# Hybrid encoder layer on one core: the down-projection of the 1024-token sequence as seven block products

## The chip, the cores and the metric

The program runs on one core of a Trainium2 chip. The metric is the device time of one execution in microseconds, lower is better. The engines of the core are TensorE (PE; its weight loads are listed as PEld), VectorE (DVE), ScalarE (ACT), GpSimd (POOL) and SyncE (SP), which here issues nearly all DMAs.

## The reference, cut to what matters

One encoder layer is applied, with the same parameters, to a prompt of 256 tokens and a sample of 1024 tokens. The change concerns its last part, the gated feed-forward network:

```
h2 = rmsnorm(x, pre_ffn_norm)
a, gate = split(h2 @ w_ffn_up, 2)          # 1024 -> 2 x 2816 features
a = centred_depthwise_conv(a, w, b)        # three taps along the tokens
f = gelu(a) * gate                         # 2816 features
x = x + rmsnorm(f @ w_ffn_down, post_ffn_norm)   # 2816 -> 1024
```

All of it is float32. Before it come the norm, the input projections, windowed attention, a bidirectional mLSTM, their gated merge and an output projection, which are as they were.

## The kernel before

Activations are kept transposed, features on partitions, tokens in columns; both sequences stand side by side as 1280 columns. A matrix product in float32 is made of three float32r matmuls: an operand is split into a high part (a rounded copy) and a low part (operand minus high), and high x high, high x low and low x high are added in PSUM. The helper `dense` (L2808) issues these three for every tile of 128 features: L2816, L2817 and L2818. So a weight that is loaded needs its high part (ScalarE, `unit_hi_ffn`, L1319) and its low part (GpSimd, `unit_lo`, L1232, which overwrites the raw weight in place), and an activation from DRAM likewise its high part (ScalarE, `pair_hi`, L1518) and its low part (DVE, `pair_lo`, L2649).

**Up stage.** 22 items, one for each tile of 128 of the 2816 features, each with the a and the gate columns of that tile. Six tiles of the first token half are done ahead, in the front; the 16 items that follow cover both halves of the tokens (c = 0 and 1), the last six, called lone items here, only the second. An item already uses the seven-product scheme with a 2 x 2 division: sums of weights are made by DVE (`block_sums`, L2548 to L2551, `last_block_sum`, L2558), the sums of operands exist. Each item is seven products of 12 matmuls per half (320 or 322 columns). DVE and ScalarE evacuate and add products (L2664, L2682, L2692, L2701), and do the convolution (L2514, L2517), gelu (L1403) and gating (L2710, L2711). SP then stores f to DRAM (`store_f`).

**Down stage.** f comes back from DRAM in three groups of tokens, `GROUPS_DOWN`: columns 0 to 400, 400 to 840 and 840 to 1280. For each group and each of eight output tiles k, `down_part` (in three parts of 8, 8 and 6 feature tiles) adds up 22 x 3 matmuls of 400 or 440 columns. In the last group the third parts stand behind all others, and those of output tiles 4 to 7 are made in two pieces of 224 and 216 columns. A weight unit of 8 tiles (512 KB) is loaded for every part and group again, through a ring of four slots (`ffn_slot`, `load_ffn`, L964): SP issues the load when the unit four before has been used. The chain behind a load is ScalarE's high part, GpSimd's low part, TensorE.

The outputs are evacuated and squared by ScalarE, the squares added by DVE (L2715), summed over features by a matmul against ones (L3347, L3375), and ScalarE makes the norm's factor of the sum (Ln and Exp, L1583 and L1585). DVE scales and adds the residual (`final`, `final_last`, L2726 to L2769), for the last group with GpSimd's help (L1309), and SP stores.

**What sets the order.** Every engine's program is written out by hand, in sequence. Engines wait for one another by semaphores; SP issues its DMAs in the order of its program, and a wait in it holds back all later ones. SP's DMAs are one queue (q1).

## Time and profile before

| | |
|---|---|
| three runs | 2429.69, 2430.98, 2431.22 us |
| median | 2430.98 us |
| profiled execution, span from first to last instruction | 2428.8 us |
| its own device time | not listed apart; the three runs lie 0.9 to 2.4 us above the span |
| TensorE busy, of the span | 98% |
| GpSimd, DVE, ScalarE busy | 51%, 55%, 38% |
| DMA moved | 245.23 MB, 101 GB/s on average |

In the profile the engines' busy times come first, then 40 slices of the span, DMA queues, the chain of work that ended last, and groups of instructions by line with what ended the idle time before them. Timelines list instructions by start; a matmul's record reaches over the start of the next one, so its length is not its cost, and the distance of starts is. In tables by stretch each engine's busy time is followed by the number of its instructions in brackets.

### The profile page before, as it was taken

How to read it: one execution, taken by the hardware profiler on the slowest of the kernel's cores; microseconds unless marked ns; L12 is line 12 of the kernel's file. 1: busy time of each engine (PE TensorE's matmuls, PEld its weight loads, DVE VectorE, ACT ScalarE, POOL GpSimd, SP SyncE). 2: the span in 40 equal slices, each digit the busy share in tenths (PEclk: the TensorE clock that was granted, in tenths of full speed). 3: DMA queues.
4: the chain of work that ended last, by engine and by line, in shares of the span. 5: the costliest groups of instructions: out<-in, count | busy, mean ns of one | idle time of the engine just before them, and what ended most of it. 6: DMA issues, size and time to landing. Idle time of an engine off the chain costs nothing.

```text
span 2428.8 us, 36204 instructions
## 1 busy us (share of the span) xinstructions
PE 2390.4 (98%) x13658; PEld 2179.4 (90%) x13658; DVE 1333.2 (55%) x2368; ACT 912.9 (38%) x1865; POOL 1238.1 (51%) x1548
## 2 busy tenths in 40 slices
PE   7999999999999999999999999999999999999998
PEld 6888888888888888888888899999999999999997
DVE  6623467334662356544776634997656568723323
ACT  5212444224432244324543112554333434543432
POOL 3145530445205641165544368795545456977664
PEclk9999999999999999999999999999999999999999
DMA  3133211321113211223355444332222224465552
GB/s 136 51 102 92 68 38 27 107 94 48 41 37 104 89 51 31 78 77 122 122 165 165 139 148 146 104 109 72 71 71 66 72 68 136 140 212 179 193 179 91
DMA packets 139190, 245.23 MB, mean 101 GB/s; under 512 B 11768, under 2 KB 85848, under 8 KB 139016
## 3 DMA queue, kind: packets, MB, share of 16 engines
q1 hardware_dynamic: 99368, 215.76, 26.8%
q10 hardware_dynamic: 39648, 27.15, 4.2%
q8 instruction: 109, 1.79, 0.3%
q14 instruction: 65, 0.53, 0.1%
HBM read 186.18 MB, written 56.61 MB: 100 GB/s over the span
## 4 chain that ended last, share of the span: by engine, by line
PE 87%; DVE 6%; DVEq 2%; POOL 2%; issue 1%; ACT 1%; DMA 1%; POOLq 0%; ACTq 0%
PE ps L2816 22%; PE ps L2818 22%; PE ps L2817 21%; PE ps L2862 3%; PE ps L2864 3%; PE ps L2863 3%; PE ps L3042 2%; PE ps L2952 2%; PE ps L2967 2%; PE ps L3062 2%; PE ps L2944 1%; PE ps L3075 1%; PE ps L3076 1%; PE ps L2934 1%; POOL unit_l L1232 1%
## 5 line engine op out<-in xcount | busy, mean ns | idle before, releaser
L2816 PE MATMUL ps<-ht_h,unit_h 128*128 128x512 f32 (+1 forms) x1408 | 508.9, 361 | 0.3 <-issue 0.3
L2818 PE MATMUL ps<-ht_h,unit_l 128*128 128x512 f32 (+1 forms) x1408 | 499.0, 354 | 0.0
L2817 PE MATMUL ps<-ht_l,unit_h 128*128 128x512 f32 (+1 forms) x1408 | 498.8, 354 | 0.0
L1102 POOL TENSOR_TENSOR unit_h<-unit_raw,colt 128x256 fp32r<-128x256 f32 x320 | 203.6, 666 | 353.1 <-DMA unit_raw<-w 352.8
L1232 POOL TENSOR_TENSOR unit_l<-unit_raw,unit_h 128x256 fp32r<-128x256 f32 x312 | 275.6, 916 | 97.0 <-ACT unit_h L1319 96.5
L2818 PEld LDWEIGHTS ps<-ht_h,unit_l 128*128 128x128 f32 x1408 | 266.2, 189 | 37.1
L2816 PEld LDWEIGHTS ps<-ht_h,unit_h 128*128 128x128 f32 x1408 | 266.6, 189 | 36.2 <-issue 0.7
L2817 PEld LDWEIGHTS ps<-ht_l,unit_h 128*128 128x128 f32 x1408 | 266.6, 189 | 35.8 <-issue 0.5
L1106 POOL TENSOR_TENSOR unit_l<-unit_raw,unit_h 128x256 fp32r<-128x256 f32 x320 | 245.6, 798 | 11.7 <-issue 0.4
L2816 PE MATMUL ps<-operands,unit_h 128*128 128x320 f32 (+1 forms) x740 | 230.9, 312 | 1.5 <-POOL sum_l L1272 1.0
L2818 PE MATMUL ps<-operands,unit_l 128*128 128x320 f32 (+1 forms) x740 | 229.7, 310 | 0.0
L2817 PE MATMUL ps<-operands,unit_h 128*128 128x320 f32 (+1 forms) x740 | 229.6, 310 | 0.0
L1272 POOL TENSOR_TENSOR unit_l<-unit_raw,unit_h 128x256 fp32r<-128x256 f32 x164 | 151.4, 949 | 94.9 <-DVE unit_raw L2551 94.9
L2816 PE MATMUL ps<-f,unit_h 128*128 128x440 f32 (+3 forms) x552 | 193.1, 350 | 0.9 <-POOL unit_l L1232 0.9
L2817 PE MATMUL ps<-f,unit_h 128*128 128x440 f32 (+3 forms) x552 | 192.4, 349 | 0.0
L2818 PE MATMUL ps<-f,unit_l 128*128 128x440 f32 (+3 forms) x552 | 192.3, 348 | 0.0
L1272 POOL TENSOR_TENSOR sum_l<-sum_raw,sum_h 128x256 fp32r<-128x256 f32 x132 | 133.1, 1028 | 101.4 <-DVE sum_raw L2558 87.0
L1148 POOL TENSOR_TENSOR bw<-bw,mask 128x256 f32<-128x256 f32 x40 | 29.3, 735 | 288.9 <-DMA bw<-exponent_rows_scratch 288.8
L1319 ACT ACTIVATE unit_h<-unit_raw 128x1024 fp32r<-128x1024 f32 (+1 forms) x84 | 83.4, 997 | 174.6 <-DMA unit_raw<-w 174.6
L2816 PE MATMUL ps<-operands,sum_h 128*128 128x320 f32 (+1 forms) x456 | 142.1, 312 | 1.4 <-POOL sum_l L1272 1.4
L2816 PEld LDWEIGHTS ps<-operands,unit_h 128*128 128x128 f32 x740 | 139.5, 188 | 3.7 <-POOL unit_l L1272 2.3
L2818 PE MATMUL ps<-operands,sum_l 128*128 128x320 f32 (+1 forms) x456 | 141.5, 310 | 0.0
(341 smaller groups left out, 5434.5 us busy)
## 6 DMA issues: line engine op xcount, KB each, us to landing
unit_raw<-w SPq DMA_DIRECT2D x197, 512.0 KB, 3.6
bw<-exponent_rows_scratch ACTq DMA_DIRECT2D x40, 256.0 KB, 3.8
unit_raw<-w SPq DMA_DIRECT2D x24, 384.0 KB, 3.0
f_raw<-f_scratch SPq DMA_DIRECT2D x10, 880.0 KB, 5.3
gate_scratch<-g_st SPq DMA_DIRECT2D x28, 256.0 KB, 3.6
f_scratch<-cv SPq DMA_DIRECT2D x22, 320.5 KB, 2.2
ym_scratch<-y_st ACTq DMA_DIRECT2D x40, 128.0 KB, 1.9
ya_scratch<-ya_st ACTq DMA_DIRECT2D x40, 128.0 KB, 2.5
```

Source lines behind the costliest of these rows:

```text
L1102: nc.gpsimd.tensor_tensor(unit_h[:, slot, k:k + 2], unit_raw[:, slot, k:k + 2], one_col.unsqueeze(2).to_broadcast([P, 2, P]), ALU.mult)
L1106: last = nc.gpsimd.tensor_tensor(unit_l[:, slot, k:k + 2], unit_raw[:, slot, k:k + 2], unit_h[:, slot, k:k + 2].bitcast(F32), ALU.subtract)
L1232: last = nc.gpsimd.tensor_tensor(unit_l[:, slot, k:k + 2], unit_raw[:, slot, k:k + 2], unit_h[:, slot, k:k + 2].bitcast(F32), ALU.subtract)
L1272: last = nc.gpsimd.tensor_tensor(lo[:, k:k + 2], raw[:, k:k + 2], hi[:, k:k + 2].bitcast(F32), ALU.subtract)
L1319: nc.scalar.activation(unit_h[:, slot, 0:k], unit_raw[:, slot, 0:k], ACT.Identity).then_inc(s_wh, 1)
L2816: mm(out_ap, wh, hi(k + k_first), start=first and k == 0, stop=False, skip_group_check=skip)
L2817: mm(out_ap, wh, lo(k + k_first), start=False, stop=False, skip_group_check=skip)
L2818: ins = mm(out_ap, wl, hi(k + k_first), start=False, stop=last and k == kts - 1, skip_group_check=skip)
L2862: mm(ps[:, bank, :], ht_h[:, k, t], unit_h[:, 0:4, k], start=k == 0, stop=False)
L2863: mm(ps[:, bank, :], ht_h[:, k, t], unit_l[:, 0:4, k], start=False, stop=False)
L2864: ins = mm(ps[:, bank, :], ht_l[:, k, t], unit_h[:, 0:4, k], start=False, stop=k == KT - 1)
L2952: ins = mm(ps[:, 3 + d, 0:DH + 1], qw[:, d, dt], c_st[:, d, dt], start=False, stop=dt == 1)
```

## The change

Only the down stage is new, and what prepares it. The prompt's 256 columns stay a direct product. The sample's 1024 tokens are halved (512 columns, `BT`), features are taken in pairs of tiles (even and odd, `HT` = 11 pairs) and output tiles in pairs p and p + 4 (`PAIRS` = 4). That is a 2 x 2 by 2 x 2 product: A11, A12, A21, A22 are blocks of the weight (even and odd feature tiles against output tile p, then against p + 4), B11, B12, B21, B22 of f (even and odd tiles, first and second token half). Seven products replace eight: A11 B11, A12 B21, S1 T1, S2 T2, S4 B22, S3 T3, A22 T4, where S1 = A21 + A22, S2 = S1 - A11, S3 = A11 - A21, S4 = A12 - S2 and T1 = B12 - B11, T3 = B22 - B12, T2 = B22 - T1, and T4 from B21 and T2.

1. **Token sums (T).** The sums are made by DVE from f as it lies in DRAM and go back to DRAM (`side_sum_scratch`). A round takes one feature pair and half of its columns: two loads into `stage`, four additions of 256 columns, one store of 512 KB. Six pairs and the weight sums of p = 0, 16 rounds, are made in the up stage, one round per item from item 1 to 16 (`ROUNDS`); the other five pairs, ten rounds, in the down stage, two per step (`ROUNDS_LATE`).
2. **First part of the down stage, by feature pairs.** Twelve steps: for each p, slices of 3, 4 and 4 feature pairs (`SLICES`). A step loads two units, the A21 and A22 tiles of the slice and the A11 and A12 tiles. TensorE makes the prompt's product with both (12 matmuls of 256 columns for a feature pair) and A11 B11 and A12 B21 with the second (6 of 512). While the raw weights are there, DVE makes S1 to S4 of the slice (`weight_sums`, eight additions, from step 2 on) and SP stores them (`weight_sum_scratch`); GpSimd may write a unit's low part over it only after the sums that read it.
3. **Second part, product by product.** Twenty blocks (`BLOCKS_DOWN`): for each of S1 T1, S2 T2, S4 B22, S3 T3, A22 T4, the four p, one block of 11 tiles from DRAM in three places of their own, 33 matmuls of 512 columns; ScalarE makes its high part, GpSimd its low part (six subtractions). The last two blocks are made in two halves of 256 columns. Token operands come in pieces (`SIDE_PIECES`, `piece_hi`, `piece_lo`) into two areas in turn.
4. DVE adds products from PSUM to what is kept in SBUF; squares, sums and norms are made as before by groups (prompt, second token half, first half in two quarters).
5. In lone items 1 to 3, and at the end of the last item, pieces of 1536, 2048 or 512 columns are split in place of pairs of 800. Four pieces more (4096 columns) follow the last item on ScalarE and DVE.

The diff, cut to its core:

```diff
-GROUPS_DOWN = [(0, 400), (400, 840), (840, T)]
...
+HT = FT // 2
+PAIRS = KT // 2
+BT = (T - SEQ_A) // 2
+HALF = BT // 2
+SUBS = [*range(FRONT // 2, HT), *range(FRONT // 2)]
+SLICES = [(0, 3), (3, 7), (7, HT)]
+STEPS = PAIRS * len(SLICES)
+U_END = U_DOWN + 2 * STEPS
+BLOCK_AT = {"A11": 0, "A12": 1, "A21": 2, "A22": 3}
+S_POS = {"S2": 0, "S4": 1, "S3": 2, "S1": 3}
+T_POS = {"T1": 0, "T3": 1, "T4": 2, "T2": 3}
+DOWN = [("S1", "T1"), ("S2", "T2"), ("S4", "B22"), ("S3", "T3"), ("A22", "T4")]
+BLOCKS_DOWN = PAIRS * len(DOWN)
...
+ROUNDS = [("S", 0, 2), ("S", 2, 4)] + [("T", m, r) for m in range(6) for r in range(2)] + [("S", 4, 6), ("S", 6, 7)]
+ROUNDS_LATE = [("T", m, r) for m in range(6, HT) for r in range(2)]
+LATE_FIRST = 2
+FIRST_SUMS = 2
+
...
+            def load_round(rounds, r, n):
+
+                kind, a, b = rounds[r]
+                if kind == "S":
+                    sp.dma_start(stage[n][:, :, 0:(b - a) * P], wdn[0, :, :, a * P:b * P].rearrange("b p c -> p b c")
+                                 ).then_inc(s_tl, 16)
+                    return
+                for k in range(2):
+                    src = f_d[2 * SUBS[a] + k, :, SEQ_A:T].rearrange("p (h r t) -> p h r t", h=2, r=2)
+                    sp.dma_start(stage[n][:, 2 * k:2 * k + 2], src[:, :, b]).then_inc(s_tl, 16)
...
+            def store_sums(n):
+
+                p, (a, b) = n // len(SLICES), slice_of(n)
+                for h, (c, d) in enumerate(((a, a + 2), (a + 2, b))):
+                    sp.wait_ge(w_sum, sums_done(n, 2 + h))
+                    sp.dma_start(s_d[p, :, :, c * P:d * P].rearrange("b p c -> p b c"), s_stage[h][:, :, 0:(d - c) * P]
+                                 ).then_inc(s_sst, 16)
...
+            for n in range(3, STEPS):
+                load_ffn(U_DOWN + 2 * n)
+                store_sums(n - 1)
+                load_ffn(U_DOWN + 2 * n + 1)
+                m = n - 2 - LATE_FIRST
+                if 0 <= m < late:
+                    for h in range(2):
+                        store_round(ROUNDS_LATE, 2 * m + h, h)
+                if 0 <= m + 1 < late:
+                    sp.wait_ge(s_tst, stored_rounds(len(ROUNDS), m + 1))
+                    for h in range(2):
+                        load_round(ROUNDS_LATE, 2 * (m + 1) + h, h)
...
+                if j >= U_DOWN + 2 * FIRST_SUMS:
+                    pool.wait_ge(w_sum, sums_done((j - U_DOWN) // 2, (1, 3)[j % 2]))
...
+            for n in range(5, 9):
+                piece_lo(n)
+            late = {0: (9,), 1: (10, 11, 12, 13, 14), 10: range(N_FIRST, N_FIRST + 3)}
+            for n in range(STEPS):
...
+                    V.tensor_tensor(x11, x12, x11, ALU.subtract)
+                    V.tensor_tensor(x12, x22, x12, ALU.subtract)
+                    dve.drain()
+                    V.tensor_tensor(x22, x22, x11, ALU.subtract)
+                    dve.drain()
+                    V.tensor_tensor(x21, x21, x22, ALU.subtract).then_inc(v_ts, 1)
...
+            def weight_sums(n):
+
+                a, b = slice_of(n)
+                ns = b - a
+                jb, jt = U_DOWN + 2 * n, U_DOWN + 2 * n + 1
+                bottom, top = unit_raw[:, ffn_slot(jb)], unit_raw[:, ffn_slot(jt)]
+                for j in (jb, jt):
+                    dve.wait_ge(s_unit[ffn_slot(j)], ffn_landed(j))
+                if n > FIRST_SUMS:
+                    dve.wait_ge(s_sst, 32 * (n - FIRST_SUMS))
+
+                def at_pos(h, name):
+                    return s_stage[h][:, S_POS[name], 0:(min(2, ns - 2 * h)) * P].rearrange("p (k c) -> p k c", c=P)
+
+                spans = ((0, 2), (2, ns))
+                for h, (c, d) in enumerate(spans):
+                    V.tensor_tensor(at_pos(h, "S1"), bottom[:, c:d], bottom[:, ns + c:ns + d], ALU.add)
+                    last = V.tensor_tensor(at_pos(h, "S3"), top[:, c:d], bottom[:, c:d], ALU.subtract)
+                last.then_inc(w_sum, 1)
+                dve.drain()
...
+                m = n - LATE_FIRST
+                if 0 <= m < len(ROUNDS_LATE) // 2:
+                    for h in range(2):
+                        stage_sums(ROUNDS_LATE, 2 * m + h, h, sum(round_dmas(r) for r in ROUNDS) + 4 * (m + 1))
+                if n == STEPS - 1:
+                    for k in range(N_FIRST + 3, N_FIRST + 7):
+                        piece_lo(k)
+                if n % 3 == 2:
+                    p = n // 3
+                    dve.wait_ge(s_used, ffn_used(U_DOWN + 2 * n + 1))
+                    dve.wait_ge(g_act, by_scalar(p))
+                    V.tensor_tensor(c11[:, p], ps[:, 6 + p % 2], k0[:, p], ALU.add).then_inc(g_dve, 1)
+                if n + 2 < STEPS:
+                    weight_sums(n + 2)
...
-            for g in range(3):
-                for k in range(KT):
-                    bank = bank_down(KT * g + k)
-                    parts = 3 if g < 2 else 2
...
+                bank = p % 2
+                jb, jt = U_DOWN + 2 * n, U_DOWN + 2 * n + 1
+                unit_ready(jb)
+                out = ps[:, bank + 2, 0:SEQ_A]
+                slice_tiles(n, jb, 0, out, "fA", 0, True, False)
+                slice_tiles(n, jb, 1, out, "fA", 1, False, True).then_inc(s_used, 1)
+                unit_ready(jt)
+                out = ps[:, bank, 0:SEQ_A]
+                slice_tiles(n, jt, 0, out, "fA", 0, True, False)
+                slice_tiles(n, jt, 1, out, "fA", 1, False, True)
+                slice_tiles(n, jt, 0, ps[:, bank + 4], "B11", None, True, True)
+                slice_tiles(n, jt, 1, ps[:, bank + 6], "B21", None, True, True).then_inc(s_used, 1)
...
+            def down_block(bl, out, first, cols=slice(0, BT)):
+
+                n = bl % 3
+                name = DOWN[bl // PAIRS][1]
+                unit_ready(U_END + bl)
+                for u in range(HT):
+                    if bl % PAIRS == 0:
+                        side_piece(name, u)
+                    ins = triple(out, blk_h[n][:, u], blk_l[n][:, u], side_tile(name, u, 0)[:, cols],
+                                 side_tile(name, u, 1)[:, cols], first and u == 0, u == HT - 1)
+                return ins
```

The names at the far right of the rows below: `stage_207` and `stage_208` are the buffers of token sums, `s_stage_209` and `s_stage_210` those of weight sums, `side_...` pieces of f or T, `wdn` the down weight, 128x2x512 a unit of a four-pair slice and 128x2x384 one of three.

**SP in the down stage, before:** units are loaded as slots come free, and now and then f.

```order
L964 DMA unit_raw<-w 128x1024 [waits unit_used] x2
L996 DMA f_raw_155<-f_scratch 128x4x440 [waits f_again0,f_stored1]
L964 DMA unit_raw<-w 128x768 [waits unit_used]
L964 DMA unit_raw<-w 128x1024 [waits unit_used] x2
L996 DMA f_raw_155<-f_scratch 128x4x440 [waits f_again1]
L964 DMA unit_raw<-w 128x768 [waits unit_used]
L964 DMA unit_raw<-w 128x1024 [waits unit_used] x2
```

**SP in the down stage, changed,** from the unit loads of step 6 to the loads of the next round of token sums.

```order
L1082 DMA unit_raw<-wdn 128x2x384 [waits unit_used]
L1155 DMA weight_sum_scratch<-s_stage_209 128x4x256 [waits w_sums]
L1155 DMA weight_sum_scratch<-s_stage_210 128x4x256 [waits w_sums]
L1082 DMA unit_raw<-wdn 128x2x384 [waits unit_used]
L1147 DMA side_sum_scratch<-stage_207 128x4x256 [waits stage_sums]
L1147 DMA side_sum_scratch<-stage_208 128x4x256 [waits stage_sums]
L1137 DMA stage_207<-f_scratch 128x2x256 [waits stage_stored]
L1137 DMA stage_207<-f_scratch 128x2x256
L1137 DMA stage_208<-f_scratch 128x2x256 x2
```

Between the two unit loads of a step now stand two stores that wait for DVE's weight sums; behind them two stores that wait for its token sums, and then loads that wait until those stores have landed.

**DVE in the down stage, changed,** in the loop's turn n = 4: the second round of token sums, then the weight sums of step 6.

```order
L2892 TENSOR_TENSOR stage_208<-stage_208 128x256 [waits stage_landed]
L2893 TENSOR_TENSOR stage_208<-stage_208 128x256
L2895 TENSOR_TENSOR stage_208<-stage_208 128x256
L2897 TENSOR_TENSOR stage_208<-stage_208 128x256
L2915 TENSOR_TENSOR s_stage_209<-unit_raw 128x256 [waits weight_sums_stored,unit_landed0,unit_landed3]
L2916 TENSOR_TENSOR s_stage_209<-unit_raw 128x256
L2915 TENSOR_TENSOR s_stage_210<-unit_raw 128x128
L2916 TENSOR_TENSOR s_stage_210<-unit_raw 128x128
```

Before, DVE had only squares to add and f to split here, and nothing of it stood between a loaded weight and its low part.

**ScalarE where the down stage begins, before:**

```order
L1518 ACTIVATE f_151<-f_raw_154 128x2x400 [waits f_again2]
L1396 ACTIVATE cv_150<-a_s_148,colt 128x641 [waits f_stored1,product_read_by_vector]
L1319 ACTIVATE unit_h<-unit_raw 128x768 [waits unit_landed1]
L1319 ACTIVATE unit_h<-unit_raw 128x1024 [waits unit_landed2]
L1403 ACTIVATE cv_150<-cv_150 128x641 [waits c_conv]
L1577 ACT_TABLE_LOAD
L1319 ACTIVATE unit_h<-unit_raw 128x1024 [waits unit_landed3]
```

**and changed:**

```order
L1526 ACTIVATE unit_h<-unit_raw 128x1024 [waits unit_landed1]
L1610 ACTIVATE cv_150<-cv_150 128x641 [waits c_conv]
L1783 ACT_TABLE_LOAD
L1726 ACTIVATE side_3_159<-side_raw_3_178 128x3x512 [waits side_piece_landed2]
L1726 ACTIVATE side_1_166<-side_raw_1_185 128x512 [waits side_piece_landed0]
L1726 ACTIVATE side_3_162<-side_raw_3_181 128x3x512 [waits side_piece_landed1]
L1726 ACTIVATE side_1_168<-side_raw_1_187 128x512 [waits side_piece_landed2]
L1526 ACTIVATE unit_h<-unit_raw 128x1024 [waits unit_landed2]
```

Behind the switch of the function table the next unit's high part came at once; now four pieces stand ahead of it.

## Rows read from the trace of the kernel before

**Rows 1.** The page: engines' busy time; the chain by engine; weight loads of one line.
```profile
PE 2390.4 (98%) x13658; PEld 2179.4 (90%) x13658; DVE 1333.2 (55%) x2368; ACT 912.9 (38%) x1865; POOL 1238.1 (51%) x1548
...
PE 87%; DVE 6%; DVEq 2%; POOL 2%; issue 1%; ACT 1%; DMA 1%; POOLq 0%; ACTq 0%
...
L2818 PEld LDWEIGHTS ps<-ht_h,unit_l 128*128 128x128 f32 x1408 | 266.2, 189 | 37.1
```

**Rows 2.** Busy time by stretch; columns are PE, PEld, DVE, ACT, POOL, clock, DMA share, GB/s.
```profile
2030.00:2106.00 76.00, 73.58 (x478) 70.68 (x478) 67.74 (x84) 44.74 (x77) 67.59 (x68) 1.00 0.51 165
2150.00:2200.00 50.00, 50.00 (x278) 50.00 (x277) 18.94 (x14) 22.59 (x29) 41.20 (x46) 1.00 0.62 202
2400.00:2429.00 29.00, 18.37 (x153) 17.61 (x151) 18.43 (x41) 6.57 (x15) 11.95 (x17) 0.86 0.24 77
```

**Rows 3.** Timeline of PE: first and last matmul of the down stage; start, us, engine.
```profile
2105.96 0.35 PE L2816 MATMUL ps<-f,unit_h 128*128 128x400 f32 x1
...
2417.50 0.27 PE L2818 MATMUL ps<-f,unit_l 128*128 128x216 f32 x1
```

**Rows 4.** Timeline of PE, projections: ends of two runs of 23 matmuls.
```profile
203.23 0.39 PE L2817 MATMUL ps<-ht_l,unit_h 128*128 128x512 f32 x1
...
208.22 0.40 PE L2818 MATMUL ps<-ht_h,unit_l 128*128 128x512 f32 x1
...
209.43 0.28 PE L2817 MATMUL ps<-ht_l,unit_h 128*128 128x256 f32 x1
...
212.07 0.28 PE L2818 MATMUL ps<-ht_h,unit_l 128*128 128x256 f32 x1
```

**Rows 5.** Timeline of DVE and POOL in an item of both sequences, DVE in a lone one.
```profile
1809.34 0.48 DVE L2711 TENSOR_TENSOR cv<-cv,kept_products 128x322 f32<-128x322 f32 x1
...
1813.58 0.69 DVE L2548 TENSOR_TENSOR sum_raw<-unit_raw 128x512 f32<-128x512 f32 x1 [2.63 <-PE ps L2818]
...
1818.78 0.49 DVE L2682 TENSOR_TENSOR kept_products<-ps,kept_products 128x320 f32<-128x320 f32 x1 [3.12 <-PE ps L2818]
...
1815.74 1.43 POOL L1272 TENSOR_TENSOR unit_l<-unit_raw,unit_h 128x256 fp32r<-128x256 f32 x2 [6.67 <-DVE unit_raw L2551]
...
2086.33 1.26 DVE L2548 TENSOR_TENSOR sum_raw<-unit_raw 128x512 f32<-128x512 f32 x1
```

**Rows 6.** Groups by shape, POOL and ACT: busy us, mean ns | idle before.
```profile
L1232 POOL TENSOR_TENSOR unit_l<-unit_raw,unit_h 128x256 fp32r<-128x256 f32 x264 | 219.1, 862 | 87.1 <-ACT unit_h L1319 87.0
...
L1319 ACT ACTIVATE unit_h<-unit_raw 128x1024 fp32r<-128x1024 f32 x48 | 50.8, 1061 | 110.6 <-DMA unit_raw<-w 110.6
```

**Rows 7.** Timeline of DVE, lone items: the same evacuation in three items.
```profile
2033.11 0.49 DVE L2664 TENSOR_TENSOR kept_products<-ps,kept_products 128x322 f32<-128x322 f32 x1 [0.16 <-issue]
...
2045.03 0.49 DVE L2664 TENSOR_TENSOR kept_products<-ps,kept_products 128x322 f32<-128x322 f32 x1 [0.67 <-PE ps L2818]
...
2058.69 0.49 DVE L2664 TENSOR_TENSOR kept_products<-ps,kept_products 128x322 f32<-128x322 f32 x1 [0.16 <-issue]
```

**Rows 8.** Timeline of DVE where the down stage begins.
```profile
2104.79 8.60 DVE L2649 TENSOR_TENSOR f<-f_raw,f 128x800 fp32r<-128x800 f32 x6
...
2117.50 1.03 DVE L2711 TENSOR_TENSOR cv<-cv,kept_products 128x322 f32<-128x322 f32 x1
```

**Rows 9.** Busy time by stretch: 1 KB rows, 2 KB and more, 1.6 KB and more.
```profile
0.00:5.00 5.00, 0.00 (x0) 0.00 (x0) 0.51 (x18) 1.28 (x1) 1.93 (x11) 1.00 0.53 148
10.00:15.00 5.00, 1.19 (x2) 0.50 (x2) 4.17 (x9) 3.04 (x5) 4.86 (x7) 1.00 1.04 399
2088.00:2091.00 3.00, 3.00 (x22) 3.00 (x22) 2.82 (x5) 1.88 (x5) 1.77 (x3) 1.00 0.96 335
```

**Rows 10.** DMA issues: how many, KB each, median us to landing.
```profile
unit_raw<-w SPq DMA_DIRECT2D x197, 512.0 KB, 3.6
...
f_scratch<-cv SPq DMA_DIRECT2D x22, 320.5 KB, 2.2
...
y_c<-ya_scratch SPq DMA_DIRECT2D x1, 1024.0 KB, 5.7
```

800 lines of the change are left out of this document (488 added, 312 removed).

## The prediction

> **What bounds the kernel now.** I read the page first: busy shares, clock, chain of waits. TensorE is busy for 98% of the span, and 87% of the chain that ended last is its own [rows 1]. The stage table then shows that only two places are not pure TensorE: the last items of the up stage (73.58 of 76 us busy) and the end (18.37 of 29 us) [rows 2]; the granted clock is 1.00, the 2.4 GHz level, where work is dense. So time is saved by removing matmul time and lost wherever an operand comes late.
>
> Busy time misleads for matmuls, since their records overlap; I read starts. In the projections 22 intervals between matmuls of 512 columns take 4.99 us, 0.227 each, and 22 of 256 columns 2.64 us, 0.120 [rows 4]: width divided by 2.4 per ns, and 13 ns on top. The down stage runs from 2105.96 to 2417.50 [rows 3], one matmul more to 2417.6: 311.7 us.
>
> **Matmuls of the down stage.** Before, the loops issue 1656, of 400, 440 and at the end 224 and 216 columns; with width / 2.4 and 13 ns they would take 95, 194 and 15 us, so 304 of the 311.7 are matmuls and some 8 are gaps, statistics and small excess. The measured 311.7 is what the new stage is set against.
> After, straight from the loops: each of 12 steps handles 3 or 4 feature pairs, each with 12 matmuls of 256 columns and 6 of 512: 12 x 0.120 + 6 x 0.227 = 2.80 us, so steps of 8.4 or 11.2 us, 4 x 30.8 = 123.2 us. Then 18 blocks of 33 x 0.227 = 7.49 us, and two blocks cut in halves, 132 x 0.120 = 15.8: 150.6 us. With five statistics matmuls, some 1.2 us, 275.0 us. If nothing is late the stage is **36.7 us shorter** than 311.7.
>
> **The up stage, both sequences.** Fifteen rounds of token and weight sums are put into DVE, four additions of 256 columns each. No row has exactly this addition. 512 columns alone take 0.69 and 322 alone 0.48 [rows 5], so 256 are near 0.41; beside GpSimd 512 took 1.26 [rows 5], so 256 some 0.65. A round is 1.6 to 2.6 us plus two drains. Just after its place DVE idles 3.12 us, before it 2.63 [rows 5], and TensorE reads its results later still. Cost: nothing, 0 to 2 us; with that cover gone it would be 15 x 2.2. SP now waits for the sums between its two weight loads, but the second load waits for the item's last product anyway.
>
> **Lone items.** Here DVE sets the pace: without an f subtraction 11.92 us pass from one L2664 to the next, with one 13.66 [rows 7]; TensorE needs 84 matmuls of 322 columns, 0.147 each, 12.4. The new pieces are 1536 columns. At the rate of six subtractions of 800 columns in 8.60 us [rows 8] one is 2.75 us, at that of 512 columns alone in 0.69 [rows 5] 2.1; I take 2.7, the row of the same operation. Three items become 1.2 us longer, one loses its subtraction (13.6 to 12.4, -1.2), the first is 1.2 longer by the last weight round (four additions of 128 columns): **+3.6** (0 to 5).
>
> **Entering the down stage.** Let t = 0 be its first matmul. Before, the six f subtractions of 8.60 us stood ahead of the last convolution [rows 8]; now 2560 columns, 4.6 us, stand there and 4096, 7.3 us, behind. On ScalarE four pieces (4096 columns, at 1.061 us per 1024 [rows 6] 4.2 us) stand ahead of the high half of step 1's second unit, ready at 10.3; GpSimd adds four subtractions, 3.8: 14.1 against 11.3 needed, 2.8 late. Step 2's second unit is loaded behind 1.5 MB of pieces that wait for the last item's f: 1.2 more. Step 3 starts at 34.8 in place of 30.8: **+4.0** (1 to 9).
>
> **The late sums, the term that decides.** In each of five turns of its loop (n = 2 to 6) DVE stands, in order, at: two rounds of token sums, which wait for four loads; then the weight sums of two steps ahead, without which GpSimd may not overwrite the unit, without which TensorE has no low half. SP stands at: weight load, two stores, weight load, two stores of token sums; then it waits until these have landed, and issues the next four loads; all that stands behind them in its program waits too. One lap is therefore: loads, sums, stores, and all share one queue. Bytes of a lap of 4 pairs: 1.05 MB each of weights, weight sums out, f in, token sums out. Rates by rows [rows 9]: rows of 1 KB, 148 GB/s at share 0.53, or 279; rows of 1.6 KB and more, 335 at 0.96, or 349; rows of 2 KB and more, 399. For 1 KB rows I take 310, between the first two; 349 to 399 for weights. 3.15/0.310 + 2.8 = 13.0 us, and 2.2 us of latency where the queue is empty (512 KB land after 3.6 us [rows 10], of which 1.4 is transfer at 384): 15.2; with a step of 3 pairs in it 14.5. Three such laps: 44.2. **Bounds of one lap:** 13.1 (all at 399, 10.9 us) and 17.9 (all at 279, and sums of 5.6 us).
> The first stores go out when step 2 is done and step 4's unit is ordered; the first loads behind them start 7.5 later. Last sums done: step 3's start + 7.5 + 44.2 + 9.5 (1 MB in, as 1024 KB of 1 KB rows took 5.7 [rows 10], and 3.8 of sums). Then 2.2 until the queued unit landed, 1.7 and 3.5 + 3.6 (four GpSimd subtractions each, 0.86 [rows 6]) and 8.3 of matmuls: step 9 starts 80.5 after step 3, not 61.6. **+18.9** (14 to 28).
> The Trainium skill (DMA: Bandwidth & Descriptors, Specifications) puts the HBM limit of a core at about 358 GB/s; the trace contradicts it, 399 in a stretch of 5 us. By the page's figure a lap would be estimated at 13.9, and the sum 3 us lower.
>
> **The rest.** DVE sums step 8's products before it makes the weight sums of step 10, 1 us late, as is block 0 by its load (704 KB 4.2, ScalarE 1.4, GpSimd 5 against 11.2): **+2** (0 to 5). In the block part GpSimd needs 4.8 of 7.49 us per block, a token operand is 5632 columns, at most 11 us of DVE in 30; nothing there is late. DVE writes the two outputs' partial sums one block after each product, banks are free for three. Cover gone, each late block costs its lateness once. At the end the last 8 outputs have 256 columns in place of 216; before, 11.2 us pass from the last dense matmul [rows 3] to the end of the span: **+0.6** (0 to 2).
>
> **Sum.** -36.7 + 3.6 + 4.0 + 18.9 + 2.0 + 0.6 = -7.6, on the profiled span of 2428.8: 2421.2. The three times lie 0.9 to 2.4 us above that span, the median 2.2. Forecast: 2430.98 - 7.6, rounded to 2423.5 us.
>
> **Rivals.**
> A, the queue is faster than I make it. With every row at 399 GB/s and stores that pass loads a lap is its 10.9 us of bytes; three are 33, the first round's 7.5, the 9.5 and the 2.2 shrink by some 5.7, and step 9 starts 63.6 after step 3: late by 2 instead of 18.9. For it: DMA was 0.62 busy in the old down stage's densest stretch [rows 2]. Against it: demand rises to some 370 GB/s, mostly 1 KB rows. What then binds is DVE beside GpSimd. From rows: DVE's 16 additions x 0.41 and GpSimd's 8 x 0.72 (two alone in 1.43 [rows 5]), if they exclude each other, need 12.4 of 11.2 us in a step of 4 and 10 of 8.4 in one of 3, 7 us over five steps: 2430.98 - 26.5 + 7 = 2411.5; with lap and port between, 2405 to 2418.
> The Trainium skill (SBUF — State Buffer, section "SBUF: two separate sides") says just this: a DVE instruction with two SBUF inputs and a GpSimd one exclude each other for the whole instruction. By that rule the 7 us are a floor; without it A would be 2406. The trace agrees that they slow each other (512 columns on DVE 0.69 alone, 1.26 beside GpSimd [rows 5]).
> B, slower than before: the same lap, longer. Every us on a lap is paid three times. At 17.2 us nothing is left of the gain, from 18.9 the kernel is measurably slower, and at 20 it is 2431 - 7.6 + 16 = 2439. It would take stores to DRAM that land 5 us later than loads of their size. Against it: f's stores of 320 KB land in 2.2 us [rows 10].
> C, the change does not shorten TensorE: if 256-column matmuls ran at the weight load's 189 ns [rows 1], 660 x 0.069 = 45 us would come back, 2469. The rows at 0.120 exclude it [rows 4].
>
> **Chances.** Forecast, 2418 to 2428: 0.37. A and port, 2405 to 2418: 0.31. Between forecast and B, 2428 to 2436: 0.13. B and other lateness, above 2436: 0.19. C under 0.01. A measurement of this kernel tells apart about 0.2%, 4.9 us. Faster by more: A and seven tenths of the forecast, 0.56; within: 0.24; slower: 0.20. The range reaches from inside A, 2407, to inside B, 2438, leaving a tenth on either side.
>
> **What would show it.** Right: dense matmuls 1518 in the stage, 0.227 and 0.120 apart; the stage near 300 us instead of 312; lone items 14.8 us apart; in the stretch from 35 to 120 us after its start TensorE waits for GpSimd's `unit_l`, GpSimd for DVE's weight sums, DVE for `stage` loads, laps near 15 us, DMA share over 0.8. Wrong: the steps of 8.4 and 11.2 us run unbroken (A); laps of 19 or more (B); gaps in the block part or in the items with both sequences, which I cost at nothing.

## The result and the profile after

| | before | after |
|---|---|---|
| median of the runs shown with the result, us | 2430.56 (2429.69 to 2431.22) | 2442.9 (2441.14 to 2443.7) |
| ratio | | 1.0048, 95% interval 1.0036 to 1.0061 |
| span of the profiled execution, us | 2428.8 | 2440.9 |
| TensorE busy, us | 2390.4 [rows 1] | 2367.4 |

The change makes the kernel **12 us slower**; forecast were 7.5 us less, and the time lies 5 us above the upper end of the range. The page of the kernel after (engines' busy time; the chain by engine):

```profile
PE 2367.4 (97%) x13522; PEld 2130.6 (87%) x13522; DVE 1455.8 (60%) x2564; ACT 901.8 (37%) x1821; POOL 1217.4 (50%) x1492
...
PE 80%; DVE 8%; DMA 4%; DVEq 3%; POOL 2%; ACT 2%; issue 1%; SPq 0%; ACTq 0%; POOLq 0%
```

TensorE is busy for 23 us less than in [rows 1], as the change wants it, and VectorE for 123 us more. In the chain TensorE falls from 87% to 80%, and DMA rises from 1% to 4%. The stretches of the down stage say where (columns: PE, PEld, DVE, ACT, POOL busy, granted clock, DMA share, GB/s):

```profile
2113.00:2150.00 37.00, 30.81 (x182) 27.43 (x182) 29.19 (x38) 16.94 (x18) 22.02 (x22) 0.95 0.71 241
2150.00:2200.00 50.00, 42.47 (x253) 38.08 (x251) 23.88 (x52) 8.60 (x13) 17.37 (x22) 0.93 0.82 269
2200.00:2250.00 50.00, 42.20 (x255) 38.55 (x256) 22.94 (x47) 10.39 (x13) 24.71 (x32) 0.90 0.71 231
2290.00:2330.00 40.00, 40.00 (x178) 33.14 (x177) 20.68 (x28) 15.06 (x15) 28.52 (x34) 1.00 0.62 214
2400.00:2441.00 41.00, 26.55 (x176) 23.79 (x174) 28.48 (x50) 6.88 (x13) 14.96 (x21) 0.91 0.34 121
```

Where [rows 2] had 50.00 of 50 us busy, TensorE is now busy for 42.47 and 42.20, and at a **granted clock of 0.93 and 0.90**, not 1.00: not only gaps, but slower matmuls. Its timeline gives the corners of the stage, the start of step 3 (2149.94) and the two longest stalls (start, us, engine; in brackets the wait before it and what ended it):

```profile
2110.79 0.28 PE L3610 MATMUL ps<-side,unit_h 128*128 128x256 f32 x1
...
2149.94 0.28 PE L3610 MATMUL ps<-side,unit_h 128*128 128x256 f32 x1
...
2174.90 0.58 PE L3610 MATMUL ps<-side,unit_h 128*128 128x256 f32 x1 [3.82 <-POOL unit_l L1439]
...
2204.75 0.58 PE L3610 MATMUL ps<-side,unit_h 128*128 128x256 f32 x1 [7.39 <-POOL unit_l L1439]
...
2269.29 0.39 PE L3610 MATMUL ps<-side,block_h 128*128 128x512 f32 x1
...
2428.28 0.28 PE L3612 MATMUL ps<-side,block_l 128*128 128x256 f32 x1
```

The stage begins 4.8 us later than in [rows 3]. Its twelve steps take 2269.29 - 2110.79 = **158.5 us**, for which the loops need 123.2. Step 3 begins 39.2 us after the start of the stage. The blocks take 159.1, to the end of their last matmul (its start and 0.12), where the loops and the statistics need 151.8. From the start of that matmul to the end of the span it is 12.6 us, before 11.3 [rows 3]. Who waits for whom in the steps (waits of PE, DVE and SP, the last two in 2113 to 2250 and 2130 to 2215; total, times, longest):

```profile
PE ps L3610 <- POOL unit_l L1439: 24.5, 9, 7.4
...
DVE s_stage L2915 <- DMA unit_raw<-wdn: 24.5, 9, 5.9
DVE stage L2892 <- DMA stage<-f_scratch: 21.3, 4, 6.2
...
SPq L1147 <- DVE stage L2897: 21.2, 8, 4.3
SPq L1137 <- DMA side_sum_scratch<-stage: 17.5, 4, 5.5
```

That is the chain foretold: TensorE for GpSimd's low halves, VectorE for the stage's loads and for weight units, SP for the token sums and then for their stores to land. SP's loads of the stage show the laps:

```profile
2157.06 1.90 SPq L1137 DMA_DIRECT2D stage<-f_scratch  x4
...
2172.41 1.90 SPq L1137 DMA_DIRECT2D stage<-f_scratch  x4
...
2186.81 1.90 SPq L1137 DMA_DIRECT2D stage<-f_scratch  x4
...
2202.23 1.90 SPq L1137 DMA_DIRECT2D stage<-f_scratch  x4
```

Laps of 15.35, 14.40 and 15.42 us, 45.2 for the three: 15.2 and 14.5 each, 44.2 in all, were forecast. So the laps are nearly as predicted, and the time is not. The matmuls say what was not in the sum. A run of 48 matmuls of 256 columns takes 5.76 us; after the stalls ending at 2174.90 and 2204.75 it takes 8.41 and 7.30, with this clock just behind them:

```profile
2205.00:2208.00 3.00, 3.00 (x15) 3.00 (x16) 0.00 (x0) 0.00 (x0) 2.45 (x4) 0.50 0.78 220
2175.00:2178.00 3.00, 3.00 (x14) 3.00 (x15) 0.00 (x0) 0.00 (x0) 2.60 (x4) 0.50 0.83 230
```

0.50 of full is the 1.2 GHz level. Five stalls (2.67, 3.12, 3.18, 3.98, 7.55 us) are followed by such a spell, which costs 1.59, 1.49, 1.51, 2.65 and 1.54 us over its run (what the run takes over its bare time): 8.8 us. All gaps of the steps sum to 25.9.

### The profile page after: what moved, and what is told of

It reads as the page before. It is cut to its first block, busy times and chain, and to the rows that moved or that the text cites. A ratio compares the mean times of both kernels' runs of the same rounds, so it can differ in the third digit from the quotient of the medians.

```text
span 2440.9 us, 36214 instructions
## 1 busy us (share of the span) xinstructions
PE 2367.4 (97%) x13522; PEld 2130.6 (87%) x13522; DVE 1455.8 (60%) x2564; ACT 901.8 (37%) x1821; POOL 1217.4 (50%) x1492
## 4 chain that ended last, share of the span: by engine, by line
PE 80%; DVE 8%; DMA 4%; DVEq 3%; POOL 2%; ACT 2%; issue 1%; SPq 0%; ACTq 0%; POOLq 0%
PE ps L3109 17%; PE ps L3111 17%; PE ps L3110 17%; PE ps L3155 3%; PE ps L3157 3%; PE ps L3156 3%; PE ps L3335 2%; PE ps L3245 2%; PE ps L3260 2%; PE ps L3355 2%; PE ps L3610 2%; PE ps L3612 2%; PE ps L3611 2%; PE ps L3237 1%; DMA unit_raw<-wdn 1%
## 5 line engine op out<-in xcount | busy, mean ns | idle before, releaser
L1307 POOL TENSOR_TENSOR unit_h<-unit_raw,colt 128x256 fp32r<-128x256 f32 x320 | 204.0, 667 | 352.4 <-DMA unit_raw<-w 352.0
L1311 POOL TENSOR_TENSOR unit_l<-unit_raw,unit_h 128x256 fp32r<-128x256 f32 x320 | 244.5, 795 | 11.7 <-issue 0.4
L1479 POOL TENSOR_TENSOR unit_l<-unit_raw,unit_h 128x256 fp32r<-128x256 f32 x164 | 155.8, 975 | 94.8 <-DVE unit_raw L2776 94.8
L1479 POOL TENSOR_TENSOR sum_l<-sum_raw,sum_h 128x256 fp32r<-128x256 f32 x132 | 140.8, 1085 | 94.4 <-DVE sum_raw L2783 79.0
L1439 POOL TENSOR_TENSOR unit_l<-unit_raw,unit_h 128x256 fp32r<-128x256 f32 x136 | 135.9, 1031 | 82.9 <-DVE s_stage L2916 68.2
L3109 PE MATMUL ps<-operands,sum_h 128*128 128x320 f32 (+1 forms) x456 | 142.4, 312 | 6.0 <-POOL sum_l L1479 6.0
L3109 PEld LDWEIGHTS ps<-operands,unit_h 128*128 128x128 f32 x740 | 139.5, 189 | 3.8 <-POOL unit_l L1479 2.4
L3110 PE MATMUL ps<-operands,sum_h 128*128 128x320 f32 (+1 forms) x456 | 141.1, 309 | 0.0
L3110 PEld LDWEIGHTS ps<-operands,unit_h 128*128 128x128 f32 x740 | 139.5, 189 | 0.1
L3111 PEld LDWEIGHTS ps<-operands,unit_l 128*128 128x128 f32 x740 | 139.4, 188 | 0.0
L2129 ACT ACTIVATE prob<-prob,small 128x384 f32<-128x384 f32 (+1 forms) x160 | 89.8, 563 | 115.5 <-DVE small L2493 115.5
```

The source lines that it names most:

```text
L1307: nc.gpsimd.tensor_tensor(unit_h[:, slot, k:k + 2], unit_raw[:, slot, k:k + 2], one_col.unsqueeze(2).to_broadcast([P, 2, P]), ALU.mult)
L1311: last = nc.gpsimd.tensor_tensor(unit_l[:, slot, k:k + 2], unit_raw[:, slot, k:k + 2], unit_h[:, slot, k:k + 2].bitcast(F32), ALU.subtract)
L1439: last = nc.gpsimd.tensor_tensor(unit_l[:, slot, k:k + 2], unit_raw[:, slot, k:k + 2], unit_h[:, slot, k:k + 2].bitcast(F32), ALU.subtract)
L1479: last = nc.gpsimd.tensor_tensor(lo[:, k:k + 2], raw[:, k:k + 2], hi[:, k:k + 2].bitcast(F32), ALU.subtract)
L2129: nc.scalar.activation(prob[:, r, a:b], prob[:, r, a:b], ACT.Exp, bias=small[:, 20 + r:21 + r], scale=HD ** -0.5, accum_out=small[:, 24 + ...
L3109: mm(out_ap, wh, hi(k + k_first), start=first and k == 0, stop=False, skip_group_check=skip)
```

## The experiments

**1 to 4: is it the late sums, and what in them?** Four kernels. The first leaves the late rounds out (pairs 6 to 8 and 8 to 11 of the T operands are loaded from the sums of other pairs):

```diff
-ROUNDS_LATE = [("T", m, r) for m in range(6, HT) for r in range(2)]
+ROUNDS_LATE = []
```

> The ten late rounds of token sums (pairs 6 to 10) are left out with their loads and stores; the four T operands take the sums of other pairs there. Theory 1 (the chain of laps: loads, sums, stores, and all the weight sums behind it, starves TensorE, and each long stall also costs a spell of the lower clock): nearly all of the 35.3 us of lateness in the steps goes, 158.5 us becomes 126 to 131, the granted clock stays 1.00, and the time is 2442.9 - 30 = 2413 (2409 to 2418). Rival 2 (it is the weight sums of the steps, their DVE work and stores, and the late rounds only lie beside them): the steps stay over 145 us, the time over 2430. The 7 us of the block part stay under both.

Measured: **2424.99 us** (0.9977 of before, 0.9967 to 0.9987), steps 139.2 us. So the late rounds cost 158.5 - 139.2 = 19.3 us in the steps, 17.9 in the medians. (The steps of one profiled execution are uncertain by some us: the two kernels with pauses below run the same steps and took 140.5 and 136.4, with three spells of lowered clock and with one, where this one has two.) But 16.0 us of lateness stay without them, where Theory 1 left 3 to 8; the time is 12 us over its centre. Its timeline has three stalls at the entry and one in step 11, all for GpSimd:

```profile
2123.70 0.39 PE L3610 MATMUL ps<-side,unit_h 128*128 128x256 f32 x1 [1.76 <-POOL unit_l L1439]
...
2133.68 0.39 PE L3610 MATMUL ps<-side,unit_h 128*128 128x256 f32 x1 [1.38 <-POOL unit_l L1439]
...
2139.83 0.39 PE L3610 MATMUL ps<-side,unit_h 128*128 128x256 f32 x1 [3.02 <-POOL unit_l L1439]
...
2239.82 0.58 PE L3610 MATMUL ps<-side,unit_h 128*128 128x256 f32 x1 [2.91 <-POOL unit_l L1439]
```

The second keeps every transfer, and SP's waits for loads and stores to land, and takes VectorE out of the lap; what it stores is raw f:

```diff
-                if 0 <= m < len(ROUNDS_LATE) // 2:
+                if 0 <= m < 0:
...
-                sp.wait_ge(v_ts, r + 1 + (len(ROUNDS) if rounds is ROUNDS_LATE else 0))
+                if rounds is ROUNDS_LATE:
+                    sp.wait_ge(s_tl, 16 * (sum(round_dmas(q) for q in ROUNDS) + 4 * (r // 2 + 1)))
```

> The late rounds are loaded and stored again as before, the same bytes in the same queue and with the same waits of the queue for loads and stores, but VectorE neither waits for them nor adds (the stored sums are raw f). If VectorE standing in order at the late loads is what starves the weight sums, the steps fall to about 135 us and the time to 2420 (2414 to 2426). If the volume of transfers, or the queue that waits for stores before it issues the next weight load, is the cause, the steps stay near 155 us and the time near 2438 (2434 to 2443).

Measured: 2441.4 us (1.0046, 1.0031 to 1.0061), steps 155.8. Almost nothing comes back. After a first lap of 16.4 us its laps are:

```profile
2174.58 1.90 SPq L1137 DMA_DIRECT2D stage<-f_scratch  x4
...
2189.31 1.90 SPq L1137 DMA_DIRECT2D stage<-f_scratch  x4
...
2204.11 1.90 SPq L1137 DMA_DIRECT2D stage<-f_scratch  x4
```

14.7 and 14.8 us without a single addition. The stores are issued some 2 us sooner behind the stage's loads, and the median one lands after 6.9 us in place of 4.8. **The lap is the queue's, not VectorE's.** So it stood in the prediction: its 13.0 us are bytes alone, 3.15 MB at 310 GB/s and 1.05 MB of weights in 2.8 us, with 2.2 us of latency and no sums.

The third gives the lap two more buffers, in the upper halves of `c21` and `c11`, which are not written before step 8 is done (ScalarE waits there for the last stores); the second pair counts its loads on a semaphore of its own, and the bytes stay the same:

```diff
-    stage = [at(f"stage{n}", o, [P, 4, 2 * P]) for n, o in enumerate((206976, 16384))]
+    stage = [at(f"stage{n}", o, [P, 4, 2 * P]) for n, o in enumerate((206976, 16384, 184320, 192512))]
...
                 if 0 <= m < late:
+                    if 0 < m < late - 1:
+                        sp.wait_ge(s_tst, stored_rounds(len(ROUNDS), m))
+                        for h in range(2):
+                            load_round(ROUNDS_LATE, 2 * (m + 1) + h, 2 * ((m + 1) % 2) + h)
                     for h in range(2):
-                        store_round(ROUNDS_LATE, 2 * m + h, h)
-                if 0 <= m + 1 < late:
-                    sp.wait_ge(s_tst, stored_rounds(len(ROUNDS), m + 1))
-                    for h in range(2):
-                        load_round(ROUNDS_LATE, 2 * (m + 1) + h, h)
+                        store_round(ROUNDS_LATE, 2 * m + h, 2 * (m % 2) + h)
+                if m == -1:
...
+                    for h in range(4):
+                        load_round(ROUNDS_LATE, h, h)
```

> Two more stage buffers, so that the loads of one lap no longer wait until the stores of the lap before have landed; same bytes, same sums. Theory 1: a lap shrinks from about 15 us to about the larger of the transfers (10 to 11 us) and VectorE's work, and the first two rounds come together; steps 135 to 145 us, time 2425 (2418 to 2432). If the transfers' volume is the limit: less than 4 us gained, 2439 to 2443.

Measured: **2427.68 us** (0.9991, 0.9982 to 1.0000), steps 140.6, 1.4 us more than with no late rounds at all, less than the same steps vary from one execution to another. Same bytes, and the queue is denser (DMA share 0.94 where the change has 0.82):

```profile
2150.00:2200.00 50.00, 46.40 (x298) 41.43 (x297) 39.45 (x67) 10.23 (x14) 26.45 (x30) 1.00 0.94 314
...
2161.24 2.92 SPq L1138 DMA_DIRECT2D stage<-f_scratch  x4
...
2173.25 2.87 SPq L1138 DMA_DIRECT2D stage<-f_scratch  x4
```

12.0 us from load to load. The volume was not what made the lap 15 us long: each load waited for the landing of the stores before it, while a fifth of the DMA engines' time went unused.

The fourth turns the order on VectorE round:

```diff
-                m = n - LATE_FIRST
-                if 0 <= m < len(ROUNDS_LATE) // 2:
-                    for h in range(2):
-                        stage_sums(ROUNDS_LATE, 2 * m + h, h, sum(round_dmas(r) for r in ROUNDS) + 4 * (m + 1))
...
                 if n + 2 < STEPS:
                     weight_sums(n + 2)
+                if 0 <= m < len(ROUNDS_LATE) // 2:
+                    for h in range(2):
+                        stage_sums(ROUNDS_LATE, 2 * m + h, h, sum(round_dmas(r) for r in ROUNDS) + 4 * (m + 1))
```

> In each step VectorE makes the weight sums first and the late token sums behind them. Theory 1 (the lap as a whole, in one queue): the weight sums come earlier once, but the token sums then start later, their stores too, and the next weight loads stand behind these stores: little changes, 2437 to 2446. If the order on VectorE alone is the cause (its waits for the stage's loads hold the weight sums up): the steps fall to about 140 us and the time to 2425 (2418 to 2430).

Measured: **2488.89 us** (1.0244, 1.0227 to 1.0261), steps 204.0. Both expectations missed it. The weight sums of step n + 2 wait for units that SP orders only just ahead of the store of the token sums; with these sums behind them, a unit's load and its sums become part of the lap:

```profile
DVE s_stage L2915 <- DMA unit_raw<-wdn: 62.9, 7, 16.4
...
2165.98 1.90 SPq L1137 DMA_DIRECT2D stage<-f_scratch  x4
...
2191.53 2.48 SPq L1137 DMA_DIRECT2D stage<-f_scratch  x4
...
2214.99 1.90 SPq L1137 DMA_DIRECT2D stage<-f_scratch  x4
```

Laps of 25.6 and 23.5 us, 9 to 11 more each, paid in every lap, with stalls of 11 to 15 us. The rival B of the prediction ("every us on a lap is paid three times") has its mechanism here, though not in the change.

**5 and 6: does a stall cost more than itself?** On the kernel without late rounds, pauses of known length ahead of seven blocks; in the second kernel TensorE fills three of them.

```diff
+                if bl in PAUSES:
+                    act.wait_ge(s_used, ffn_used(U_END + bl))
+                    for _ in range(PAUSES[bl]):
+                        nc.scalar.activation(pause[:, 0:512], pause[:, 512:1024], ACT.Copy)
+                        act.drain()
+                    act.sem_inc(s_pause, 1)
...
+                if bl - 1 in PAUSES:
+                    for _ in range(FILL.get(bl - 1, 0)):
+                        x = side_tile("B22" if q == 2 else DOWN[q][1], 0, 0)
+                        mm(ps[:, 2 * p + (q not in (0, 2))], x[:, 0:P], x, start=True, stop=True)
+                    pe.wait_ge(s_pause, sum(k < bl for k in PAUSES))
```

> The kernel without late rounds, and in its block part seven pauses made on purpose: after the blocks 2, 8, 10, 4, 12, 6 and 14 TensorE waits until ScalarE has made 2, 3, 5, 7, 9, 13 and 25 copies of 512 columns (some 0.6 us each: about 1.3, 2, 3.2, 4.4, 5.6, 8 and 15.5 us). Theory 1: the short pauses cost themselves and nothing more, the next block takes 7.5 us; behind those of 3 us and more the granted clock is at its lower level for a spell and the next block takes 9 to 10.5 us. The rival (a stall costs only itself, and the slow matmuls in the steps come from memory traffic): every block takes 7.5 us, whatever stands before it.

> As the kernel with pauses, but TensorE fills those after the blocks 2, 4 and 6 with 4, 15 and 28 matmuls of 512 columns whose results nobody reads (0.9, 3.4 and 6.4 us at 0.227). Theory 1: the idle rest is under 2 us each time and the next block takes 7.5 us, while the unfilled pauses still cost their 1.5 to 3 us each. Rival (it is the length of the wait at the semaphore or the neighbour's traffic, not TensorE's idleness): the blocks after the filled pauses are as slow as in the kernel with pauses.

Measured: 2483.38 and 2474.83 us, one run each. In the kernel with pauses, the time that the two blocks behind each pause took (66 matmuls; 15.04 us behind the shortest):

| TensorE idle, us | 1.80 | 2.34 | 3.73 | 5.29 | 6.80 | 9.46 | 17.67 |
|---|---|---|---|---|---|---|---|
| two blocks behind it, us | 15.04 | 15.07 | 16.69 | 17.27 | 17.20 | 17.55 | 16.86 |
| more than bare | 0 | 0 | 1.7 | 2.2 | 2.2 | 2.5 | 1.8 |

The rows of the kernel with pauses, behind 2.34, 3.73 and 5.29 us of idling:

```profile
2345.00:2350.00 5.00, 4.50 (x20) 3.76 (x21) 3.00 (x2) 3.76 (x4) 0.65 (x2) 1.00 0.67 255
2364.00:2369.00 5.00, 4.70 (x14) 3.74 (x15) 0.69 (x1) 2.19 (x3) 2.91 (x5) 0.66 0.01 6
2298.00:2303.00 5.00, 4.12 (x10) 3.28 (x11) 2.78 (x2) 4.89 (x5) 0.09 (x1) 0.50 0.83 300
```

(The stall of 1.80 was ended by GpSimd's low half and not by its pause.) With fills the pause after block 4 left 1.70 us idle, and the two blocks took 15.10 in place of 17.27; the one after block 6 left 2.94, where under 2 were expected, and they took 16.7. Windows of that kernel behind both:

```profile
2293.00:2298.00 5.00, 4.51 (x20) 3.74 (x21) 2.96 (x2) 4.89 (x5) 0.27 (x1) 1.00 0.78 288
2317.00:2322.00 5.00, 4.12 (x12) 3.30 (x13) 0.00 (x0) 2.12 (x3) 2.63 (x4) 0.71 0.23 74
```

ScalarE's copies and the transfers are the same in both kernels; only TensorE's own idleness differs. So a long stall costs itself and one spell at the lower level, here 1.7 to 2.5 us, once, however long it was.

The seven pauses suggest a sharp edge between 2.34 and 2.94 us. The other stalls of these kernels don't show one. Two executions that ran the same steps, the kernel without late rounds and the one with filled pauses, had stalls of 3.18 and 3.15 us at the same place; only the first was followed by the lower clock:

```profile
2139.90:2142.90 3.00, 3.00 (x17) 3.00 (x18) 2.83 (x8) 1.72 (x2) 1.36 (x2) 0.61 0.06 21
```

```profile
2139.90:2142.90 3.00, 3.00 (x25) 3.00 (x26) 2.83 (x8) 1.84 (x2) 1.29 (x2) 1.00 0.07 27
```

And the first stall of the down stage, 1.92 to 1.95 us, cost nothing more in four kernels and 1.6 us in three (weight sums first, both with pauses). Over all kernels here, stalls under 1.9 us with dense work behind them cost at most some 0.5 us more, those of 3.46 us and more always 1.4 to 2.8, and those between sometimes the one and sometimes the other; what decides is open. The Trainium skill (TensorE: Matmul & The Clock Gate, "HAM oscillation — how this bites in real kernels") says that gaps in a kernel throw the clock back to half and the matmuls behind them pay. For stalls of 3.46 us and more the trace agrees, with these 1.4 to 2.8 us; for those of 1.92 to 3.43 us it does in some executions and not in others.

**7 to 11: what are the 16 us that stay?** First, on four stage buffers, two orders at the entry:

```diff
+            unit_hi_ffn(act, U_DOWN + 3)
             for n in range(5, 9):
                 piece_hi(n)
-            unit_hi_ffn(act, U_DOWN + 3)
...
             load_ffn(U_DOWN + 4)
+            load_ffn(U_DOWN + 5)
             sp.wait_ge(s_f[1], stored(1, ITEMS - 1))
             for n in range(12, N_FIRST):
                 load_piece(n)
-            load_ffn(U_DOWN + 5)
```

> Four stage buffers, and the entry to the down stage in another order: ScalarE makes the high half of the fourth weight unit ahead of four side pieces, and the sixth unit is loaded ahead of three pieces that wait for the last item's f. The three stalls there were 1.92, 1.09 and 3.18 us, the last followed by some 1.7 us of lowered clock. Theory: they fall to 2 us in all, the clock stays up, and the time is 2427.7 - 5.5 = 2422 (2419 to 2425). Rival: the transfers are the limit there and the pieces come late in their place; 2426 to 2429.

Measured: 2425.14 us (0.9977, 0.9967 to 0.9986), half of what was expected, and not clear of the interval of the kernel with four buffers alone. The first stall went, the second is 0.55 us; the third stayed, 3.17, as did the spell behind it. Then two orders of VectorE:

```diff
             add_square_y(("C21", 1))
-            final(1, range(4, KT))
+            final(1, (4,))
...
             last_part(0)
+            final(1, (5, 6))
             last_part(1)
             add_square_y(("C21", 2, 0))
             add_square_y(("C21", 3, 0))
+            final(1, (7,))
             last_part(2)
...
             for n in range(STEPS):
+                if n == 10:
+                    dve.wait_ge(s_split, U_B + B_UP0 + ffn_used(U_DOWN + 2 * STEPS - 1) - 2 * KT)
                 for k in late.get(n, ()):
                     piece_lo(k)
```

> As the kernel before it in this list, and two more orders of VectorE: the last partial sums of the two outputs stand between the final additions of the second group rather than behind them (the statistics matmul waited 2.8 us for them), and the first side pieces of the block part wait until GpSimd has made the last low halves of the steps (eight subtractions took 10.4 us beside them, 6.4 without; TensorE waited 3.2 us and ran 1.5 us at a lowered clock behind it). Theory: 2.5 + 4.2 us less than the kernel before it, 2415.5 (2412 to 2419). Rival: the pieces are now late for block 0 and the final additions for the end; 2420 or more.

Measured: 2421.44 us (0.9962, 0.9948 to 0.9976), 3.7 less than the kernel before it and not 6.7; the two intervals overlap, and the two profiled executions are equally long (2425.0 and 2425.3). The trace shows no gain in the tail. From the end of the third half block to the end of the span it is 20.1 us, where the change has 19.8; the 22.9 of the kernel before it in this list hold a spell of lowered clock (0.57 from 2405 to 2412). The wait of the third statistics matmul fell from 2.84 to 1.19 us, and that of the last rose from 2.3 to 3.7. The stall in step 11 (3.61 us) is gone too, and one of 3.25 us stands at block 0: both moved. That spoke for a limit in the work of two engines. GpSimd's rows in the change:

```profile
2238.49 6.38 POOL L1439 TENSOR_TENSOR unit_l<-unit_raw,unit_h 128x256 fp32r<-128x256 f32 x8 [7.49 <-DVE s_stage L2916]
2249.01 10.37 POOL L1439 TENSOR_TENSOR unit_l<-unit_raw,unit_h 128x256 fp32r<-128x256 f32 x8 [4.15 <-DVE s_stage L2916]
```

The same eight subtractions take 6.38 us with no side piece of VectorE's beside them and 10.37 with three; its weight sums stand beside both. So the ninth kernel, without late rounds, leaves out VectorE's low halves of the pieces 5 to 18 (ten at the entry, four at step 11; TensorE reads the high halves in their place):

```diff
             def piece_lo(n):
                 _, a, b, m = SIDE_PIECES[n]
                 dve.wait_ge(t_hi, piece_hi_done(n))
+                if 5 <= n < N_FIRST + 4:
+                    dve.sem_inc(d_lo, 1)
+                    return
```

> The kernel without late rounds, and VectorE leaves out the low halves of the side pieces at two places: the ten at the entry to the down stage and the first four of the block part (TensorE reads the high halves there in their place). GpSimd's subtractions are untouched. What is left without late rounds were 16 us over the bare matmuls in the steps. Theory 3 (at both places it is VectorE's pieces that stand before its weight sums and slow GpSimd's subtractions beside them): eight subtractions take 6.4 us again in place of 9.8 to 10.4, both stalls of some 3 us and the lowered clock behind them go, the steps take 127 to 130 us and the time is 2425.0 - 10 = 2415 (2411 to 2418). Rival (the weight units' transfers come late there): the steps stay over 135 us, the time over 2421.

Measured: **2416.33 us** (0.9945, 0.9931 to 0.9959), steps 130.8, 0.8 above the range of Theory 3 and far from the rival's 135. GpSimd's group of subtractions in 2115 to 2250, first without late rounds, then without the pieces' lows too (min/median/max ns):

```profile
L1439 POOL TENSOR_TENSOR unit_l<-unit_raw,unit_h x80: 717/908/2252, 2114.1 to 2239.0; 128x256 fp32r<-128x256 f32 x80
```

```profile
L1441 POOL TENSOR_TENSOR unit_l<-unit_raw,unit_h x80: 725/752/994, 2114.5 to 2230.6; 128x256 fp32r<-128x256 f32 x80
```

The median falls from 908 to 752 ns and the longest from 2252 to 994, with GpSimd's program unchanged. Half of the 16 us is VectorE's piece subtractions. They could do it by standing ahead of its weight sums or by slowing GpSimd; the rows of the two kernels tell these apart. Without late rounds (VectorE's first weight sum of step 2 and its five pieces behind; GpSimd's low halves of step 1's second unit, of step 2, of step 11):

```profile
2128.46 0.42 DVE L2915 TENSOR_TENSOR s_stage<-unit_raw 128x256 f32<-128x256 f32 x1 [2.54 <-DMA unit_raw<-wdn]
...
2132.97 7.36 DVE L2875 TENSOR_TENSOR side<-side_raw,side 128x512 fp32r<-128x512 f32 x5
...
2119.92 3.73 POOL L1439 TENSOR_TENSOR unit_l<-unit_raw,unit_h 128x256 fp32r<-128x256 f32 x4 [3.83 <-ACT unit_h L1526]
2130.04 9.74 POOL L1439 TENSOR_TENSOR unit_l<-unit_raw,unit_h 128x256 fp32r<-128x256 f32 x8 [6.39 <-DVE s_stage L2916]
...
2229.40 10.36 POOL L1439 TENSOR_TENSOR unit_l<-unit_raw,unit_h 128x256 fp32r<-128x256 f32 x8 [4.12 <-DVE s_stage L2916]
```

Without the pieces' lows too:

```profile
2128.68 0.43 DVE L2920 TENSOR_TENSOR s_stage<-unit_raw 128x256 f32<-128x256 f32 x1 [12.80 <-DMA unit_raw<-wdn]
...
2120.31 2.81 POOL L1441 TENSOR_TENSOR unit_l<-unit_raw,unit_h 128x256 fp32r<-128x256 f32 x4 [3.82 <-ACT unit_h L1528]
2130.26 6.37 POOL L1441 TENSOR_TENSOR unit_l<-unit_raw,unit_h 128x256 fp32r<-128x256 f32 x8 [7.15 <-DVE s_stage L2921]
...
2224.91 6.40 POOL L1441 TENSOR_TENSOR unit_l<-unit_raw,unit_h 128x256 fp32r<-128x256 f32 x8 [3.89 <-DVE s_stage L2921]
```

The weight sums of step 2 wait for their unit to land in both and start at the same time, so the pieces did not hold them up; those of step 11 stand ahead of the pieces. What changes is GpSimd: 9.74 and 10.36 us for eight subtractions become 6.37 and 6.40. The lateness of steps 1 and 2 falls from 8.4 to 3.5 us and that of step 11 from 4.6 to 0.9. The stall at step 2's first unit stays, 2.29 us: it is that load, and this kernel does not touch it. The Trainium skill (SBUF — State Buffer, "SBUF: two separate sides") has a VectorE instruction with two SBUF inputs and a GpSimd one exclude each other for the whole instruction. By that rule the longest GpSimd subtraction beside the pieces is one that waited out a piece of 1536 columns; the trace agrees in size, 2.25 us in the kernel without late rounds, where three such pieces take 6.17, 2.06 each. Whether the engines exclude each other or only slow each other was not told apart.

Last, two kernels to run in earnest: four buffers, the entry's orders, the tail's order, and piece 9 behind the weight sums of step 2; the first of the two with the pieces of step 11 behind the first half of GpSimd's eight as well (the cut shows what both have):

```diff
-            late = {0: (9,), 1: (10, 11, 12, 13, 14), 10: range(N_FIRST, N_FIRST + 3)}
+            late = {1: (10, 11, 12, 13, 14), 10: range(N_FIRST, N_FIRST + 3)}
...
                 if n + 2 < STEPS:
                     weight_sums(n + 2)
+                if n == 0:
+                    piece_lo(9)
```

> Four stage buffers, the entry's order, the last partial sums early, and at two places another order on VectorE: the ninth side piece behind the weight sums of step 2, and the first pieces of the block part behind the first half of GpSimd's last eight subtractions. Theory 3: the stall of 3.2 us in step 2 falls under 1.5 us and the clock stays up there (4 us), that in step 11 falls from 3.6 to 1.5 without a stall at block 0 (3 us): 2425.1 - 2.9 (tail) - 4 - 3 = 2415 (2411 to 2419). Rival (the work of VectorE and GpSimd together is the limit, and an order only moves the stall): 2420 to 2423.

> As the kernel before it in this list without the last of its orders: the first pieces of the block part stand as in the change. Theory 3: 3 us slower than that one, 2418 (2415 to 2421). Rival: no difference between the two.

Measured: 2421.46 us (0.9962, 0.9948 to 0.9976) and **2420.58 us** (0.9963, 0.9950 to 0.9976). No difference between the two, and against the kernel before them in the list (2421.44) none either: the rival's numbers. In step 2 the stall fell to 2.48 us in both. The clock behind it fell in the first (0.66) and stayed up in the second, with the same orders up to there:

```profile
2137.60:2140.60 3.00, 3.00 (x18) 3.00 (x19) 2.91 (x7) 0.00 (x0) 0.18 (x1) 0.66 1.09 372
```

```profile
2136.00:2139.00 3.00, 3.00 (x25) 3.00 (x26) 2.91 (x7) 0.00 (x0) 0.20 (x1) 1.00 1.08 372
```

Step 11 still stalls for 3.2. Both beat the kernel before by 9 to 10 us and the change by 21 to 22. Against four buffers alone all the orders together are worth some 6 us, clear of the intervals; no single one of them is.

## Why the prediction was wrong

The steps of its sum against what was measured, all in us of the profiled execution:

| term | predicted | measured | from |
|---|---|---|---|
| matmuls | -36.7 | -36.7 | runs without a stall take their bare time: 5.76, 5.47 |
| lone items | +3.6 | +4.8 | start of the stage, 2110.79 |
| entering | +4.0 | +8.4 | start of step 3: 39.2 after that of the stage, bare 30.8, forecast 34.8 |
| late sums | +18.9 | +19.3 | 158.5 less 139.2 |
| rest of the steps | +2.0 | +7.6 | 35.3 less 8.4 and 19.3 |
| block part | 0 | +7.3 | 159.1 less 151.8 |
| tail | +0.6 | +1.3 | 12.6 less 11.3 |
| sum | -7.6 | +12.0 | spans: +12.1 |

**Right.** That 256 columns cost 0.120 and that rival C was out. That rounds in items of both sequences cost nothing: from 1620 to 2030 TensorE is busy for 409.51 of 410 us. The late sums, called the term that decides: the waits, the laps (45.2 us for 44.2) and the 18.9; from step 3 to step 9 it is 83.1 us, forecast 80.5, and 2.0 of this lateness stand there without late rounds too. Part of that is luck: 5.8 of the 19.3 us are lowered clock behind the stalls of 3.98, 7.55 and 2.67 us, which it had not, so it priced the gaps too high by as much. (The bytes of a lap at 399 GB/s are 10.5 us, not the 10.9 of rival A and of the lower bound; nothing in the forecast hangs on it.) That a lap's chain moves the time as said was shown in both directions, by four buffers (-15.2 us) and by the weight sums put first (+46).

**Wrong: "Entering the down stage" and "The rest".** They ran to 8.4 and 7.6 us in place of 4.0 and 2.0. The first half of the entry held: of "GpSimd adds four subtractions, 3.8: 14.1 against 11.3 needed" the four took 3.7 us, and the stall was 1.9 us where 2.8 were forecast. The step that failed is the next: "Step 2's second unit is loaded behind 1.5 MB of pieces that wait for the last item's f: 1.2 more". It let this load cost only its own lateness. In the trace VectorE's weight sums of step 2 wait for it, and GpSimd for them, so that step 2's first unit is already 1.6 us late; then GpSimd's eight subtractions stand beside 7.4 us of VectorE's pieces and take 9.7 us in place of 6.4, and the second unit is 3.2 us late, with 1.5 of lowered clock behind it. The prediction had the effect in its hands ([rows 5]: 0.69 alone, 1.26 beside) and priced it in rival A, for the sums, on the chance that nothing else was late; it left it out of the forecast at the two places with the most of both. And it put 1 us on step 10, 1 on block 0 and nothing on step 11, where three pieces cost a stall of 3.1 us and 1.5 of clock. Of these 16 us, 8.3 went when the pieces' lows were left out.

**Missing: the clock.** The windows [rows 2] show 1.00 where work is dense and 0.86 at the end; the forecast took stalls at their length. In the change 8.8 of the steps' 35.3 us of lateness are what the 1.2 GHz behind stalls cost. No term of the sum held it.

**Wrong: "nothing there is late" in the block part.** This term, put at nothing, measured 7.3 us and is the largest miss. From the timeline of the change: stalls of 0.81, 1.03 and 1.22 (for `block_l`), 0.41 behind the second statistics and 2.84 (the third statistics, for the square sums) add up to 6.3. The last is VectorE's order, four final products ahead of partial sums that a matmul needs; with another order it fell to 1.19, but the time did not come back, since the last statistics waited longer by as much. Why `block_l` is late in some blocks may be VectorE's work beside GpSimd's; that was not tried and stays open.

The cases: rival B had the right size (2439) by the wrong term; "B and other lateness, above 2436" had 0.19, and it was the other lateness.

## What to carry to other kernels

Count an added transfer not by its bytes but by the lap it stands in: buffers that are loaded, worked on and stored in place and loaded again make the queue wait for a landing, and a second pair of buffers was worth 15 us at unchanged bytes. Where a change adds work to VectorE and GpSimd at the same place, price the sum of the two and not each by its rate alone. And give every stall that is expected to be long, here from some 3.5 us on, a second price, the spell of the lower clock behind it.

## What the hardware did that was not expected

The price of a stall does not grow with it: behind 17.67 us of idling the matmuls lost 1.8 us, about as much as behind 3.73 (1.7) and less than behind 5.29 (2.2). And in the middle it is not a function of the length: 2.48 us cost 1.6 us more in one kernel and nothing in another, 3.18 and 3.15 us at the same place 1.6 and nothing. Short gaps did no harm by being many: the four-buffer kernel has five of 0.5 to 1.7 us between 2150 and 2200, and its granted clock there is 1.00 in the row above.
